# Encoder block, one core: three raw strips loaded a block earlier, the route block reordered with the first expert gather inside it, expert weight splits and a norm step moved, and unread products of the unit matrix put into TensorE's waits

## The chip, the cores and the metric

The kernel runs on one core of one Trainium2 chip. The metric is the time of one execution on the device, in microseconds (us); lower is better. The core has TensorE (PE in the profile; PEld is its weight load), VectorE (DVE), ScalarE (ACT), GpSimd (POOL) and SyncE (SP, which here only issues DMAs), and 16 DMA engines.

## The reference

A residual block over 4096 rows of width 1024, behind 16 meta rows: a norm, a mixer, a norm, a mixture of experts, a norm.

```python
h = _layernorm(jnp.concatenate([meta, x], axis=1), ln0_g, ln0_b)
mix = _mixer(h, w_in[l], ...)                      # 1024 -> 4352 wide projection, attention and convolution, w_o
h = _layernorm(alpha * h + mix, ln1_g[l], ln1_b[l])
ffn = _hier_moe(h, ...)
h = _layernorm(alpha * h + ffn, ln2_g[l], ln2_b[l])

# _hier_moe: the best of 4 groups, in it the best 2 of 8 experts
g_prob = softmax(xt @ w_rg + b_rg); g_top, g_idx = top_k(g_prob, 1)
e_top, e_loc = top_k((xt @ w_re + b_re) in the group g_idx, 2)
weight = g_top * softmax(e_top)
order = argsort(eid); sizes = bincount(eid, length=32)
xs = xt[tok[order]]
a = silu(ragged_dot(xs, w_gate, sizes)) * ragged_dot(xs, w_up, sizes)      # 1024 -> 512
ys = ragged_dot(a, w_down, sizes) * weight[order]                            # 512 -> 1024
out = zeros.at[tok[order]].add(ys)
```

Products must be as exact as fp32. The kernel gets that by splitting each fp32 operand into a rounded high part and the rest, and running three fp32r products (high by high, low by high, high by low) for each one of the reference.

## The kernel before

**Stages.** `mixer` begins with a prologue, a block of its own in which the meta rows go through the norm and the projection (its products are L564, on strips of `meta_raw`). The main block follows: 8 blocks of 512 rows (`BLOCKS`, `TOK`), each in 50 strips of weights (`N`); in the first block each strip is loaded raw from memory (`load_raw`, L636, into `raw`), its high part is made by ACT (`w_slot` L743) and its low part by DVE (L898), and it is stored split (`split_weights`), from where the later seven blocks load it. At the end of a block the eight transposes' groups that carry the next block's rows (`HX_AT`) stand one per strip. Behind the last block TensorE does for each of the last 4 row tiles `router_rows` (8 transposes) and `router_product`, and then `router_logits`; each waits for the norm's and the split's steps on DVE, POOL and ACT.

**route** turns the router's logits into lists. DVE chooses groups and experts (L84 to L122), TensorE counts them (`rank_rows`, L153 and L154, ahead of the semaphore `counted`), DVE works out the first tile of each expert (`bounds`, `tile_row`), each choice's place (`place_rows`, L169 to L174) and its weight (`weigh`, L135 to L147), writes 16 one-hot tables (L1441, L1443), which ACT scales (`listed`, L1386) and TensorE multiplies (`lists`, L1469). POOL gathers the records of the earlier blocks (`r_got`), TensorE turns them (`turned`, L1474), and DVE adds both into `row_index` (L1450 and on). SP meanwhile loads the first expert's weights (12 chunks of 512 KB: 4 gate, 4 up, 4 down), whose first 8 high parts ACT makes behind its `listed` (L1391).

**experts** runs 32 experts over 82 tiles of 128 gathered rows, laid out as a loop over the experts and in it a loop over the expert's tiles; 16 experts have 2 tiles, 12 have 3, 3 have 4 and one has 1. The engines run the same loop, joined only by semaphores. For tile `g`:

- TensorE: 24 gate products, 24 up products (each weight chunk serves 6), 8 transposes of the next tile's rows, 24 down products of tile `g-1`, 4 transposes of `prod`. Before the first tile's up products of an expert it waits for the low parts of its up chunks.
- ACT: Silu of the gate result (`act`, L1644), in an expert's last tile (`swap`) the high parts of the next expert's 4 gate chunks, the next rows' high parts (`xT_hi`), in the last tile the high parts of the 4 up chunks, `aT_hi`, in an expert's first tile the down chunks, and `measure(g-1)` (sum and sum of squares for the last norm, L1630 to L1634).
- DVE: in the last tile the 4 gate low parts of the next expert (L1673), `prod` (L1719), `xT_lo` (L1668), `normalise(g-2)` (L1688, L1693), in the last tile the 4 up low parts, `aT_lo` (L1726), `add_base(g-1)` (`both`, L1682, waits for the gathered `base`), in the first tile the 4 down low parts.
- POOL: `gather_rows(g+2)`, whose landing it waits for; `store_rows(g-2)`; `store_part(g-1)`; `deviation(g-1)` (two small steps that make 1/sigma of the norm, L1579 and L1582); a wait for the part's landing; `gather_base(g)`. `hold` is a wait in the instruction stream, so the order of these is the order of the code, and each index (`x_at`, `out_at`, `y_at`) is copied and waited for ahead of its DMA.
- SP: reloads each chunk for the next expert once its low part has been made, in the order gate, up, down.

Semaphores count; nothing is planned by a program. The order on each engine is that of the code.

## Time and profile before

| | us |
|---|---|
| median of 3 runs | 4194.5 |
| fastest and slowest of them | 4185.06 and 4198.86 |
| the profiled execution, its own time | 4199.52 |
| its span in the trace | 4197.5 |

The profiled execution took 2.0 us more than its span, and 5.0 us more than the median. The page gives each engine's busy time, the chain of work that ended last, and the costliest groups of instructions; the timeline gives single instructions with the idle time ahead of them and what ended it; the waits list who waited for whom; the windows give busy time and TensorE's granted clock by stretch (1.00 is 2.4 GHz, 0.50 is 1.2 GHz). "issue" as a releaser means that the profile shows no other engine that was waited for. The cuts used below: prologue 0 to about 62, mixer to about 2634, `route` to about 2662, `experts` to the end.

### The profile page before, as it was taken

How to read it: one execution, taken by the hardware profiler on the slowest of the kernel's cores; microseconds unless marked ns; L12 is line 12 of the kernel's file. 1: busy time of each engine (PE TensorE's matmuls, PEld its weight loads, DVE VectorE, ACT ScalarE, POOL GpSimd, SP SyncE). 2: the span in 40 equal slices, each digit the busy share in tenths (PEclk: the TensorE clock that was granted, in tenths of full speed). 3: DMA queues.
4: the chain of work that ended last, by engine and by line, in shares of the span. 5: the costliest groups of instructions: out<-in, count | busy, mean ns of one | idle time of the engine just before them, and what ended most of it. 6: DMA issues, size and time to landing. Idle time of an engine off the chain costs nothing. (4 is left out here: it accounts for less than half of the span.)

```text
span 4197.5 us, 60770 instructions
## 1 busy us (share of the span) xinstructions
PE 4076.5 (97%) x20066; PEld 3395.4 (81%) x20067; DVE 2073.1 (49%) x3202; ACT 1439.2 (34%) x2543; POOL 744.8 (18%) x1020
## 2 busy tenths in 40 slices
PE   8999999999999999999999998699999999999997
PEld 7888888888888888888888887587888888788886
DVE  3554443443443443443443444577656567665664
ACT  2422311311311311311311311366556456555553
POOL 2000010000000001001001001234333333433333
PEclk9999999999999999999999998799999999999998
DMA  8787456456456455456455555676756566665562
GB/s 251 241 306 244 145 202 204 156 198 196 159 199 195 166 200 187 169 197 187 175 197 184 175 197 186 217 254 222 252 187 205 188 219 229 228 211 190 195 218 81
DMA packets 278468, 840.53 MB, mean 200 GB/s; under 512 B 47952, under 2 KB 99408, under 8 KB 226688
## 3 DMA queue, kind: packets, MB, share of 16 engines
q1 hardware_dynamic: 228400, 716.61, 50.2%
q0 software_dynamic: 49936, 121.90, 8.7%
q8 instruction: 114, 1.87, 0.2%
q14 instruction: 18, 0.15, 0.0%
HBM read 717.60 MB, written 178.45 MB: 213 GB/s over the span
## 5 line engine op out<-in xcount | busy, mean ns | idle before, releaser
L1110 PE MATMUL bank<-hT_hi,w_slot 128*128 128x512 f32 x2176 | 862.3, 396 | 8.3 <-DVE w_slot L898 7.2
L1112 PE MATMUL bank<-hT_hi,w_slot 128*128 128x512 f32 x2176 | 848.9, 390 | 0.0
L1111 PE MATMUL bank<-hT_lo,w_slot 128*128 128x512 f32 x2176 | 848.1, 390 | 0.0
L1742 PE MATMUL e_bank<-e_w_hi,e_xT_hi 128*128 128x512 f32 x1312 | 522.7, 398 | 18.2 <-DVE e_xT_lo L1668 15.8
L1744 PE MATMUL e_bank<-e_w_hi,e_xT_lo 128*128 128x512 f32 x1312 | 514.7, 392 | 0.0
L1743 PE MATMUL e_bank<-e_w_lo,e_xT_hi 128*128 128x512 f32 x1312 | 513.9, 392 | 0.0
L1673 DVE TENSOR_TENSOR e_w_lo<-e_raw,e_w_hi 128x1024 fp32r<-128x1024 f32 x384 | 444.1, 1220 | 116.7 <-ACT e_w_hi L1624 116.7
L1110 PEld LDWEIGHTS bank<-hT_hi,w_slot 128*128 128x128 f32 x2176 | 409.0, 188 | 105.8 <-issue 24.6
L1112 PEld LDWEIGHTS bank<-hT_hi,w_slot 128*128 128x128 f32 x2176 | 408.9, 188 | 87.4
L1111 PEld LDWEIGHTS bank<-hT_lo,w_slot 128*128 128x128 f32 x2176 | 409.5, 188 | 81.2
L1624 ACT ACTIVATE e_w_hi<-e_raw 128x1024 fp32r<-128x1024 f32 x376 | 366.2, 1054 | 2.0 <-issue 2.0
L1742 PEld LDWEIGHTS e_bank<-e_w_hi,e_xT_hi 128*128 128x128 f32 x1312 | 248.3, 189 | 71.7 <-issue 22.5
L1744 PEld LDWEIGHTS e_bank<-e_w_hi,e_xT_lo 128*128 128x128 f32 x1312 | 248.1, 189 | 53.6
L1743 PEld LDWEIGHTS e_bank<-e_w_lo,e_xT_hi 128*128 128x128 f32 x1312 | 248.7, 190 | 50.0
L1742 PE MATMUL e_bank<-e_w_hi,e_aT_hi 128*128 128x512 f32 x664 | 266.5, 401 | 2.7 <-DVE e_both L1682 2.7
L52 POOL TENSOR_SCALAR rstd<-moments 128x1 f32<-128x1 f32 (+1 forms) x69 | 24.8, 359 | 1360.7 <-DVE moments L47 1360.7
L1744 PE MATMUL e_bank<-e_w_hi,e_aT_lo 128*128 128x512 f32 x664 | 260.3, 392 | 0.0
L1743 PE MATMUL e_bank<-e_w_lo,e_aT_hi 128*128 128x512 f32 x664 | 259.7, 391 | 0.0
L766 ACT ACTIVATE work<-bank 128x512 f32<-128x512 f32 x128 | 76.5, 598 | 506.9 <-PE bank L1112 506.9
L1110 PE MATMUL bank<-w_slot,mixT_hi 128*128 128x512 f32 x512 | 206.5, 403 | 0.0
L1630 ACT ACTIVATE e_ignored<-e_both 128x1024 bf16<-128x1024 f32 x83 | 87.5, 1054 | 343.8 <-DVE e_both L1682 343.8
L716 POOL COPY h_rows<-x_rows 128x1024 f32<-128x1024 f32 x32 | 33.2, 1042 | 953.9 <-PE bank L1122 941.2
(330 smaller groups left out, 6712.7 us busy)
## 6 DMA issues: line engine op xcount, KB each, us to landing
w_slot<-split_weights SPq DMA_DIRECT2D x353, 1024.0 KB, 4.8
e_raw<-in_w_exp_gate_dram SPq DMA_DIRECT2D x128, 512.0 KB, 6.0
e_raw<-in_w_exp_up_dram SPq DMA_DIRECT2D x128, 512.0 KB, 6.1
e_raw<-in_w_exp_down_dram SPq DMA_DIRECT2D x128, 512.0 KB, 5.4
split_weights<-w_slot SPq DMA_DIRECT2D x50, 1024.0 KB, 5.7
h_rows<-h_rows SPq DMA_DIRECT2D x64, 512.0 KB, 7.7
x_rows<-in_x_dram SPq DMA_DIRECT2D x32, 512.0 KB, 5.5
raw<-in_w_in_dram SPq DMA_DIRECT2D x30, 512.0 KB, 7.2
```

Source lines behind the costliest of these rows:

```text
L52: po.tensor_scalar(rstd[0:rows, :], moments[0:rows, 1:2], LN_EPS, None, ALU.add).then_inc(ln_rstd, 1)
L716: po.tensor_copy(h[:, i1, :], xs[:, i1, :]).then_inc(h_copied, 1)
L766: a.activation(w[:, 0:TOK], got, ACT.Sigmoid).then_inc(taken_act, 1)
L1110: pe.matmul(out, hi, x_hi, start=first, stop=False)
L1111: pe.matmul(out, hi, x_lo, start=False, stop=False)
L1112: return pe.matmul(out, lo, x_hi, start=False, stop=last)
L1624: a.activation(w_hi[:, c, :], raw[:, c, :], ACT.Copy).then_inc(split_count(e, c, True)[0], 1)
L1630: a.activation(ignored[:, :], both[:, :], ACT.Copy, accum_out=moments[:, 0, :]).then_inc(summed, 1)
L1673: v.tensor_tensor(w_lo[:, c, :], raw[:, c, :], w_hi[:, c, :].bitcast(FP32), ALU.subtract)\
L1742: pe.matmul(out_p, hi, x_hi, start=first, stop=False)
L1743: pe.matmul(out_p, hi, x_lo, start=False, stop=False)
L1744: return pe.matmul(out_p, lo, x_hi, start=False, stop=last)
```

## The change

1. **Prologue.** The first 3 raw strips are issued at the end of the prologue's SP queue and no longer at the head of the next block's. `meta_raw` moves to the slots' area so that `raw` is free.
2. **Mixer.** The eight groups of `HX_AT` stand in pairs, two at each second strip.
3. **route.** DVE weighs ahead of the wait for `counted`; the placing and the tables stand ahead of the writing of `bounds`; ACT makes 4 high parts ahead of `listed` and 4 behind; DVE makes 2 low parts (`done_early`) ahead of its wait for the lists; POOL gathers the first tile's rows inside `route` once `row_index`'s first column is written (`first_rows`), and no longer at the head of `experts`.
4. **experts, splits.** DVE makes the first expert's gate low parts 2 and 3 and the first `xT_lo` ahead of its six memsets. In the loop an expert's 4 up low parts move from the last tile of the expert ahead of it to the head of its own first tile; the 4 gate low parts are parted, 2 ahead of `prod` and 2 behind `xT_lo`.
5. **experts, norm.** POOL's `deviation(g-1)` moves behind `gather_base(g)`. ACT runs a Silu of one column into `e_unused` at the end of each tile.
6. **`keep_warm`.** TensorE runs fp32 products of the unit matrix by itself, 512 columns wide, into a bank that nobody reads: 6, 3, three times (2 and 2), and 1 behind the mixer (22 in all); 6, 7 and 7 in `route`; 2 behind the first transposes of `experts` and 3 ahead of the last down product. 47 in all, each number fixed.

```diff
+def keep_warm(pe, bank, ident, count):
+    for _ in range(count):
+        pe.matmul(bank[:, :], ident[:, :], ident[:, :].unsqueeze(1).to_broadcast([P, 4, P]), start=True, stop=True)
...
@@ mixer, prologue, sync
+                for s in range(RAW):
+                    for dst, src in strip_dmas(*strips[s], raw[:, s, :]):
+                        sp.dma_start(dst, src).then_inc(raw_in[s], 16)
@@ mixer
-        HX_AT = {WO0 - 1 + i: i for i in range(2 * TILES)}
+        HX_AT = {WO0 + 2 * i: (2 * i, 2 * i + 1) for i in range(TILES)}
...
-                for s in range(ahead):
-                    load_raw(s)
...
                 pe.wait_ge(hx_lo, BLOCKS * 2 * TILES + 1)
+                keep_warm(pe, pj[0], ident, 6)
                 pe.wait_ge(wo_taken, BLOCKS * 2 * TILES + 1)
                 for i in range(TILES):
+                    if i:
+                        keep_warm(pe, pj[0], ident, 2)
                     router_rows(BLOCKS, i)
+                    keep_warm(pe, pj[0], ident, 2 if i else 3)
                     router_product(BLOCKS, i)
+                keep_warm(pe, pj[0], ident, 1)
                 router_logits(BLOCKS)
@@ route, gpsimd
                 po.wait_ge(got_in, 16)
+                po.wait_ge(first_rows, 1)
+                po.tensor_copy(x_at[:, :], row_index[:, 2:3, 0]).then_inc(weights["x_at_set"], 1)
+                hold(po, weights["x_at_set"], 1)
+                po.indirect_dma_start(out=weights["rows"][:, :], out_offset=None, in_=h1[0:h1.shape[0] // 2, :],
...
@@ route, scalar
+                split_hi(range(weights["early"] // 2))
                 for j in range(2 * TILES):
...
-                for c in range(weights["early"]):
...
+                split_hi(range(weights["early"] // 2, weights["early"]))
@@ route, vector
+                v.wait_ge(exp_ready, 1)
+                weigh(v, link, r, tb)
                 v.wait_ge(counted, 1)
...
+                for c in range(weights["done_early"]):
+                    v.wait_ge(weights["hi_ready"], c + 1)
+                    v.tensor_tensor(weights["w_lo"][:, c, :], weights["raw"][:, c, :],
...
                 v.wait_ge(listed_up, 1)
@@ route, tensor
+                keep_warm(pe, spare_bank, tb["ident"], 6)
                 pe.wait_ge(both_ready, 1)
                 rank_rows(pe, r, tb, ranks, E).then_inc(counted, 1)
+                keep_warm(pe, spare_bank, tb["ident"], 7)
...
                 mm.then_inc(turned_up, 1)
+                keep_warm(pe, spare_bank, tb["ident"], 7)
@@ experts, gpsimd
-                gather_rows(0)
+                hold(po, rows_in, 16)
...
                     store_part(g - 1)
-                    deviation(g - 1)
                     hold(po, part_out, g * 16 + 16)
                     gather_base(g)
+                    deviation(g - 1)
@@ experts, scalar
                         measure(g - 1)
+                        a.activation(unused[:, :], minus_half[:, :], ACT.Silu)
@@ experts, vector
                 total = count_tiles(v)
+                for c in range(weights["done_early"], GC):
+                    split_lo(0, c)
+                evacuate(0)
...
-                for c in range(2 * GC):
-                    split_lo(0, c)
-                evacuate(0)
...
                     with v.Fori(lo, hi) as g:
+                        with v.If(g == lo):
+                            for c in range(GC, 2 * GC):
+                                split_lo(e, c)
                         with v.If(g == swap):
-                            for c in range(GC):
+                            for c in range(GC // 2):
                                 split_lo(e + 1, c)
...
                         evacuate(g * 2 + 2)
+                        with v.If(g == swap):
+                            for c in range(GC // 2, GC):
+                                split_lo(e + 1, c)
                         normalise(g - 2)
-                        with v.If(g == swap):
-                            for c in range(GC, 2 * GC):
-                                split_lo(e + 1, c)
@@ experts, tensor
                 transposes(16)
+                keep_warm(pe, bank[3], ident, 2)
...
+                keep_warm(pe, bank[3], ident, 3)
                 down(total - 1)
```

Three places as the instructions stand on their engines. DVE in the experts' loop, from `xT_lo` to the first of the two `both` of a tile, before; `e_w_lo` is a low part, the branches are the tests for the last and the first tile:

```order
L1668 TENSOR_TENSOR e_xT_lo<-e_bank,e_xT_hi 128x512
L1688 SCALAR_TENSOR_TENSOR e_done<-e_both,e_minus_mean,e_gain 128x1024
...
L1693 SCALAR_TENSOR_TENSOR e_finished<-e_done,e_rstd,e_shift 128x1024
L1722 COMPARE_AND_BRANCH
L1672 ISA
L1673 TENSOR_TENSOR e_w_lo<-e_raw,e_w_hi 128x1024
...
L1726 TENSOR_TENSOR e_aT_lo<-e_bank,e_aT_hi 128x512
...
L1682 SCALAR_TENSOR_TENSOR e_both<-e_bank,slot_weight,e_base 128x512
```

The same engine in the changed kernel, from the start of an expert to `prod`:

```order
L1559 TENSOR_LOAD bounds
L1559 ISA x2
L1743 UNCONDITIONAL_BRANCH
L1744 COMPARE_AND_BRANCH
L1702 ISA
L1703 TENSOR_TENSOR e_w_lo<-e_raw,e_w_hi 128x1024
...
L1744 UNCONDITIONAL_BRANCH
L1747 COMPARE_AND_BRANCH
...
L1703 TENSOR_TENSOR e_w_lo<-e_raw,e_w_hi 128x1024
...
L1752 TENSOR_TENSOR e_prod<-e_bank,e_act 128x512
```

The up low parts (under L1744) now stand behind the read of the new expert's `bounds`, which itself stands behind both `both` of the tile ahead.

POOL in the experts' loop, from the part's store to the end of a tile, before and then changed:

```order
L1572 DMA h_rows<-e_both,e_y_at 9216x1024
L1579 TENSOR_SCALAR e_rstd<-e_moments 128x1
L37 REGISTER_ALU
L1582 TENSOR_TENSOR e_rstd<-e_rstd,minus_half 128x1
L37 ISA
L1563 ISA
L1563 COPY e_y_at<-row_index 128x2
L1566 DMA e_base<-h_rows,e_y_at 128x1024
```

```order
L1601 DMA h_rows<-e_both,e_y_at 9216x1024
L37 ISA
L1592 ISA
L1592 COPY e_y_at<-row_index 128x2
L1595 DMA e_base<-h_rows,e_y_at 128x1024
L1608 TENSOR_SCALAR e_rstd<-e_moments 128x1
L37 REGISTER_ALU
L1611 TENSOR_TENSOR e_rstd<-e_rstd,minus_half 128x1
```

The two steps on `e_rstd` went from ahead of the wait (`L37`) for the part's landing to behind the base's DMA, at the end of the tile.

TensorE in `route`, changed (`L44` is `keep_warm`); before, the same rows stand without those of `L44`:

```order
L44 MATMUL r_spare_bank<-ident 128x512 x6
L159 MATMUL r_ranks<-lr_both,before 128x128
L160 MATMUL r_ranks<-lr_both,ones 128x128
L44 MATMUL r_spare_bank<-ident 128x512 x7
L1496 MATMUL r_lists<-r_listed,r_hot_lo 128x196 x8
L1501 MATMUL r_turned<-ident,r_got 128x128 x2
L44 MATMUL r_spare_bank<-ident 128x512 x7
```

The count of `r_ranks` now stands behind six of the unread products, and the lists behind seven.

## Rows read from the trace of the kernel before

**Rows 1.** The page: an engine's busy time and share, the chain's lines.

```profile
PE 4076.5 (97%) x20066; PEld 3395.4 (81%) x20067; DVE 2073.1 (49%) x3202; ACT 1439.2 (34%) x2543; POOL 744.8 (18%) x1020
...
DMA e_rows<-h_rows,e_x_at 8%; DMA h_rows<-e_both,e_y_at 7%; PE e_bank L1742 2%; PE e_bank L1744 2%; PE e_bank L1743 2%; POOL out_dram L1588 1%; DVE e_w_lo L1673 1%; POOL e_out_at L1586 1%; POOL e_y_at L1563 1%; DMA e_base<-h_rows,e_y_at 1%; POOL e_x_at L1555 1%; PE e_bank L1751 0%; ACT e_ignored L1630 0%; POOLq L37 0%; DVE e_both L1682 0%
```

**Rows 2.** Windows: stretch, its length, busy time of PE (x count), then PEclk.

```profile
200.00:2500.00 2300.00, 2298.98 (x11642) 1.00 0.57 193
2640.00:2653.00 13.00, 3.22 (x12) 0.50 1.02 390
2676.00:2681.00 5.00, 5.00 (x14) 0.54 1.03 404
2700.00:4170.00 1470.00, 1444.16 (x6787) 1.00 0.62 210
```

**Rows 3.** Timeline (start, length, instruction, idle before), end of the prologue.

```profile
51.65 2.72 PE L564 MATMUL bank<-work,meta_raw 128*128 128x16 f32 x12
...
55.09 4.18 SPq L636 DMA_DIRECT2D raw<-in_w_in_dram  x4
...
61.62 0.76 PE L1110 MATMUL bank<-hT_hi,w_slot 128*128 128x512 f32 x1 [7.25 <-DVE w_slot L898]
```

**Rows 4.** Waits of PE between 2600 and 2640: total us, times, longest.

```profile
PE bank L1130 <- DVE router_rowsT_lo L865: 10.0, 4, 4.1
```

**Rows 5.** Timeline of `route` and the start of `experts`.

```profile
2640.69 0.74 DVE L160 COPY lr_earlier<-base 128x32 f32<-128x32 f32 x1 [1.28 <-PE r_ranks L154]
...
2647.57 0.17 DVE L135 TENSOR_REDUCE lr_gsum<-lr_gexp 128x4 f32<-128x16 f32 x1
...
2649.34 0.27 DVE L1441 TENSOR_SCALAR r_hot_hi<-r_count_up,r_tile_of 128x98 f32<-128x98 f32 x1
...
2650.43 4.30 PE L1469 MATMUL r_lists<-r_listed,r_hot_lo 128*128 128x196 f32 x16 [9.78 <-ACT r_listed L1386]
...
2662.67 0.18 POOL L1555 COPY e_x_at<-row_index 128x1 int32<-128x1 int32 x1 [16.93 <-POOLq L1355]
...
2668.05 1.97 PE L1751 MATMUL e_bank<-ident,e_rows 128*128 128x128 f32 x8 [13.09 <-DMA e_rows<-h_rows,e_x_at]
...
2675.52 0.79 PE L1742 MATMUL e_bank<-e_w_hi,e_xT_hi 128*128 128x512 f32 x1 [5.50 <-DVE e_xT_lo L1668]
```

**Rows 6.** Waits of PE, DVE and POOL in the experts' loop, 2700 to 4170.

```profile
PE e_bank L1742 <- DVE e_xT_lo L1668: 10.3, 9, 1.2
PE e_bank L1787 <- DVE e_prod L1719: 9.2, 7, 2.9
...
DVE e_both L1682 <- DMA e_base<-h_rows,e_y_at: 88.7, 36, 5.6
...
POOL e_rstd L1579 <- ACT e_ignored L1634: 24.2, 20, 4.7
```

**Rows 7.** Timeline of PE, POOL and DVE from expert 5's first tile on.

```profile
2856.71 0.48 PE L1742 MATMUL e_bank<-e_w_hi,e_xT_hi 128*128 128x512 f32 x1
...
2857.93 1.58 POOL L1566 DMA_INDIRECT e_base<-h_rows,e_y_at  x1 [0.85 <-POOL e_y_at L1563]
...
2858.49 4.62 DVE L1673 TENSOR_TENSOR e_w_lo<-e_raw,e_w_hi 128x1024 fp32r<-128x1024 f32 x4
...
2863.63 1.40 DVE L1682 SCALAR_TENSOR_TENSOR e_both<-e_bank,slot_weight,e_base 128x512 f32<-128x512 f32 x2
...
2872.30 0.19 POOL L1579 TENSOR_SCALAR e_rstd<-e_moments 128x1 f32<-128x1 f32 x1
2872.64 0.57 POOL L1582 TENSOR_TENSOR e_rstd<-e_rstd,minus_half 128x1 f32<-128x1 f32 x1
...
2874.16 0.19 POOL L1563 COPY e_y_at<-row_index 128x2 int32 x1 [0.95 <-DMA h_rows<-e_both,e_y_at]
```

**Rows 8.** Groups by line, 2700 to 4170: ACT's table load in the loop.

```profile
L1644 ACT ACT_TABLE_LOAD x81 | 103.9, 1283 | 44.4 <-issue 43.5
```

**Rows 9.** Timeline of DVE at the kernel's end.

```profile
4181.86 1.41 DVE L1682 SCALAR_TENSOR_TENSOR e_both<-e_bank,slot_weight,e_base 128x512 f32<-128x512 f32 x2 [4.44 <-DMA e_base<-h_rows,e_y_at]
```

More of the change, by code:

```diff
@@ L326, in mixer @@
         raw = place([weights + 4 * 6 * D], "raw", [P, RAW, D])
-        meta_raw = place([weights + 4 * 4 * D], "meta_raw", [P, META_RAW, D])
+        meta_raw = place([weights], "meta_raw", [P, META_RAW, D])
         at = [weights + 4 * 8 * D]
@@ L357, in mixer @@
         tp = banks[6:8]
+        raw_in = [sem(f"raw_in{i}") for i in range(RAW)]
         with ExitStack() as c1, nc.Block() as block:
@@ L364, in mixer @@
             gains_in = sem1("gains_in")
-            raw_in = [sem1(f"meta_raw_in{i}") for i in range(META_RAW)]
+            meta_raw_in = [sem1(f"meta_raw_in{i}") for i in range(META_RAW)]
             ln_step, ln_moments, ln_rstd, ln_gained, ln_done = (
@@ L566, in _ @@
                     mm.then_inc(pj_ready, 1)
-        raw_in = [sem(f"raw_in{i}") for i in range(RAW)]
         x_in = [sem(f"x_in{i}") for i in range(TILES)]
@@ L826, in block_of_strips @@
                             take_rows(b, RT_AT[s])
-                        if s in HX_AT:
-                            q = HX_AT[s]
+                        for q in HX_AT.get(s, ()):
                             a.wait_ge(hx_ready, b * 2 * TILES + q + 1)
@@ L1071, in block_of_strips @@
                             place_rows(v, route_link, r, tb, tb["region"]).then_inc(slots_ready, 1)
-                        if s in HX_AT:
-                            q = HX_AT[s]
+                        for q in HX_AT.get(s, ()):
                             v.wait_ge(hx_hi, b * 2 * TILES + q + 1)
@@ L1270, in block_of_strips @@
                             rank_rows(pe, r, tb, quad[2], E).then_inc(counted, 1)
-                        if s in HX_AT:
-                            q = HX_AT[s]
+                        for q in HX_AT.get(s, ()):
                             pe.wait_ge(ln_done, b * LNS + TILES + q // 2 + 1)
@@ L1314, in load_expert_chunk, with route @@
     sp.dma_start(dst, expert_chunk(t, e, c)).then_inc(weights["raw_in"][c], 16)
-def route(nc, t, tb, records, keep, weights):
+def route(nc, t, tb, records, h1, keep, weights):
     G, E = t["w_rg"].shape[1], t["w_re"].shape[1]
@@ L1338, in route @@
         upto, first, spare = sb("r_upto", [P, E]), sb("r_first", [P, E]), sb("r_spare", [P, E])
+        start = sb("r_start", [P, E])
         tile_row_f, tile_row = sb("r_tile_row_f", [P, 1]), sb("r_tile_row", [P, 1], I32)
@@ L1344, in route @@
         got = sb("r_got", [P, P, 2])
-        ranks, lists, turned = [ctx.enter_context(nc.psum_tensor(name, [P, TOK], FP32))
-                                for name in ("r_ranks", "r_lists", "r_turned")]
+        ranks, lists, turned, spare_bank = [ctx.enter_context(nc.psum_tensor(name, [P, TOK], FP32))
+                                            for name in ("r_ranks", "r_lists", "r_turned", "r_spare_bank")]
         tables, step = sem("r_tables"), sem("r_step")
@@ L1388, in _ @@
                     ins.then_inc(worth_made, 1)
-                for c in range(weights["early"]):
-                    a.wait_ge(weights["raw_in"][c], 16)
-                    a.activation(weights["w_hi"][:, c, :], weights["raw"][:, c, :], ACT.Copy)\
-                     .then_inc(weights["hi_ready"], 1)
+                split_hi(range(weights["early"] // 2, weights["early"]))
             @block.vector
@@ L1423, in _ @@
                 v.tensor_tensor(tile_row[:, :], tile_row_f[:, :], tile_no[:, :], ALU.add).then_inc(tile_rows_ready, 1)
+                link(v.tensor_scalar(start[:, :], first[:, :], float(P), None, ALU.mult))
+                link(v.tensor_tensor(r["earlier"][:, :, :], r["earlier"][:, :, :],
+                                     ranks[:, 0:TILES * E].rearrange("p (t e) -> p t e", e=E), ALU.add))
+                link(place_rows(v, link, r, tb, start))
+                v.tensor_scalar(in_tile_i[:, :], tb["slot"][:, :], P - 1, None, ALU.bitwise_and)
+                link(v.tensor_scalar(tile_of_i[:, :], tb["slot"][:, :], P.bit_length() - 1, None, ALU.arith_shift_right))
+                v.tensor_copy(in_tile[:, :], in_tile_i[:, :])
+                link(v.tensor_copy(tile_of[:, :], tile_of_i[:, :]))
+                for j in range(2 * TILES):
+                    v.tensor_scalar(hot_hi[:, j, :], count_up[:, 0:MT], tile_of[:, j:j + 1], None, ALU.is_equal)\
+                     .then_inc(hi_made, 1)
+                    v.tensor_scalar(hot_lo[:, j, :], count_up[:, :], in_tile[:, j:j + 1], None, ALU.is_equal)\
+                     .then_inc(lo_made, 1)
                 v.tensor_copy(bounds[:, 0, :], first[:, :])
@@ L1824, in encoder_block @@
                        raw_in=[ctx.enter_context(nc.semaphore(f"e_raw_in{c}")) for c in range(chunks)],
+                       rows=sb("e_rows", [P, D]), x_at=x_at,
                        hi_ready=ctx.enter_context(nc.semaphore("e_hi_ready")),
+                       lo_ready=ctx.enter_context(nc.semaphore("e_lo_ready")),
+                       rows_in=ctx.enter_context(nc.semaphore("e_rows_in")),
+                       x_at_set=ctx.enter_context(nc.semaphore("e_x_at_set")),
                        consts_in=ctx.enter_context(nc.semaphore("e_consts_in")))
-        route(nc, t, tb, records, keep, weights)
+        route(nc, t, tb, records, h1, keep, weights)
         experts(nc, t, h1, out2, keep, weights, tb)
```

47 lines of the change are left out of this document (22 added, 25 removed).

## The prediction

> **What bounds the kernel now.** The page first: TensorE is busy 97% of the span, and yet most of the chain that ended last is DMA waits of POOL's gathers and stores, 8% and 7% [rows 1]. The windows by stretch say where TensorE is not the bound. From 200 to 2500 us it is busy 2298.98 of 2300 us at full clock, so nothing that other engines do in the mixer's main blocks can move the time. In the experts' loop, 2700 to 4170, it is busy 1444.16 of 1470 us [rows 2]; the tiles that nothing disturbs are 17.7 us long there, which is 72 products of 0.227 us, twelve short transposes and little else. 82 such tiles would take 1452 us; they take 1492 (2675.52 to about 4168), so 40 us are lost, of which the waits name 10.3 for `xT_lo` and 9.2 for `prod` [rows 6]; the rest is clock drops and ends. The other places are the gap of 7.25 us behind the prologue [rows 3], the mixer's tail [rows 4], and `route` with the first tile's start: 2634 to 2675.52 [rows 5], with the clock at 0.50 and 0.54 of full for most of it [rows 2].
>
> **Prologue: minus 4.0 us.** The last meta products end at 54.4, SP issues the raw strips at 55.09, and the first product follows at 61.62, 6.5 us behind the issue [rows 3]. Issued earlier, the strip is there when the block opens, and ACT's and DVE's splits (1.06 and 1.23 us) with their handovers remain: first product near 57.6. Gain 61.6 - 57.6 = 4.0, between 3 and 4.5.
>
> **HX_AT: 0 to 1 us gained.** The main blocks have 1 us idle in 2300 us [rows 2]. Pairs save some switches between product kinds; I take 0.3.
>
> **Mixer's tail: 0.** TensorE waits four times for DVE's `router_rowsT_lo`, 10.0 us in all [rows 4], and about 6 us for the last norm. What keeps DVE late is its own row of norm steps, which is untouched. The 22 unread products lie in these waits. Their cost: 16 records of 196 columns took 4.30 us, 0.27 each, on a clock of 0.50 that rose near their end [rows 2, 5]. Two records of 512 columns are then 2 x 0.27 x 512/196 = 1.4 us at that mean; I estimate 0.9 at full and 1.8 at half clock. Two of them fit a wait of 2.5 to 4 us; if they don't, they put off TensorE by under 1 us at each of four places. 0 to plus 2 us, I take 0.
>
> **route and the first tile: minus 14 us.** Three steps. (a) `weigh`, 2647.57 to 2649.34, moves into DVE's wait for the count, which ends with L160 at 2640.69 and 1.28 us of waiting [rows 5]: 1.8 us earlier, less 0.5 by which it overruns the wait, and the 0.4 of `bounds`. The lists come 1.5 us earlier. (b) The first rows' index was copied at 2662.67, behind the block's end, and the rows reached TensorE at 2668.05 [rows 5]. The copy now follows `row_index` at about 2655, so the rows are there near 2660.5 and TensorE's transposes start when `experts` opens, near 2661 instead of 2668.05. From there ACT's and DVE's split of them gives a first product at 2664.4: in the trace 7.5 us lay between, because DVE still had 8 low parts to make [rows 5]; now 2 are done and 2 stand ahead, and 3.4 us remain. 2675.5 - 2664.4 = 11.1. (c) 12 products ran at 0.43 us before the clock rose (5.00 us for 14 records at 0.54 [rows 2]); with the unread products ahead they run at 0.23, which saves 2.4. Together 13.5; against it, six unread products at half clock (1.8 each, from 2634 on) can hold the count, due at 2639.4, for 1 to 3 us. Range 10 to 15, I take 13.5 with up to 3 of it open.
>
> **The end: minus 0.7.** The last `both` waits at 4181.86 for the base [rows 9], which the part's store and `deviation` stand ahead of; with `deviation` behind it, it is issued 0.7 us sooner. The three products ahead of the last down product save TensorE a stretch at half clock, but this wait hides it.
>
> Front and end together: 4.0 + 0.3 + 13.5 + 0.7 = **18.5 us gained.**
>
> **The loop, up low parts: this is what decides.** TensorE needs the first up chunk's low part 24 x 0.227 = 5.45 us into an expert's first tile. Before, DVE had made all four before that: it starts them 1.8 us into the tile (2858.49 against 2856.71), ahead of `aT_lo` and `both` [rows 7], the first being ready at 3. Now they stand behind `both`, and so behind the base's landing. Two bounds. Without any wait for the base: `normalise` ends about 2.5 us into the tile (it ended at 1.8; two low parts less stand ahead of `prod`, which comes sooner, two stand behind `xT_lo`), then `aT_lo` 0.65, both 1.4, reading the new bounds 1.1, the first low part 1.15: 6.8, a stall of 1.3 us. 31 changes of expert give 40 us. With the base as it lands now: it is issued 1.22 us into the tile at 2857.93 [rows 7] and takes 4.8 us in the median of all of its DMAs, so `both` starts at 6.0 at the earliest, the low part is ready at 9.7, and TensorE stalls 4.2. Over the 31 changes (their rows are those of L1566 and L1742 like the two shown) the issue lies between 8 us ahead of the tile and 1.4 us into it; 10 changes give the floor of 1.3, the other 21 give their landing less 1.85, and the sum is 81 us. DVE's 36 waits for the base, 88.7 us [rows 6], show that it is late often; before, TensorE had until 10 us into the tile before that reached it.
>
> **The loop, deviation.** Its two steps (0.19 and 0.57 us, from 2872.30 to 2873.21) lay under the part's landing, which ended at 2874.16 [rows 7]. Behind the base they add 0.9 us with the hold to POOL's own row of steps, and that row is already as long as TensorE's tile: by the mean of all tiles 18.2 us of index copies, issues and landings, with 0.9 us of it waiting for others. Nothing is queued behind the base but the next tile's row gather, whose landing POOL waits for, and so the next base. If POOL sets the pace everywhere this is 82 x 0.9 = 74 us; if TensorE's stalls let POOL catch up, or where an expert's middle tiles leave it 3 us, it is nothing by itself. What it saves is the wait for ACT's sum, 24.2 us [rows 6]. It acts through the base, so it adds to the stalls above and not beside them.
>
> **Taken together.** The stalls are 40 at least and 81 with today's base. A stalled TensorE makes POOL's next base earlier by comparison, which pulls to the floor; `deviation` pulls to the top. I take 67. Against it, the first two low parts fewer ahead of `prod` remove the waits for `prod` and `xT_lo`, 9.2 + 10.3 [rows 6], and some 3 us of low clock behind them: 22. **Net 45 us lost**, between 15 (40 less 25) and 90 (81 and some 10 of `deviation`).
>
> Clock: stalls of 2 us in an otherwise full tile were followed by a fall to half speed in three of four cases of this trace, each costing 1.7 us; where POOL sets the pace it costs nothing more. It is inside the range.
>
> **ACT's Silu into `e_unused`.** ACT loads a table ahead of each tile's Silu, 81 times 1.283 us [rows 8]. On ACT's row of the changed kernel this load still stands in the loop ahead of the Silu; the added Silu costs 0.2 us at a place where ACT waits. By this row nothing is gained: 0. The Trainium skill (ScalarE: Activation LUTs, What ACT_TABLE_LOAD costs) says the load is a real instruction placed when compiling and that a switch costs its 1283 ns and a drain of about 1380 ns; the trace agrees with the first number. If the switch were avoided by that rule, Silu would come up to 2.7 us earlier, which no term of the sum uses.
>
> **The sum.** 4199.5 (profiled) - 18.5 + 45 = 4226; against the median of 4194.5, 5.0 below that execution, **4221 us**. The case's own range: 4194.5 - 15 + 90 = 4269 down to 4194.5 - 18.5 + 15 = 4191.
>
> **Rivals.** (1) The stalls don't come, the front's gain stays: *faster*. The mechanism is the base: if it lands within 3 us of the tile's start and DVE's reading of the bounds costs little, the first up part is ready at 5.5. It decides at 1.8 us: every `both` that ends 3.2 us into the tile or sooner costs nothing. For it: in 10 of 31 changes the base is there by then, and half as many splits stand ahead of `prod`. Against: the others, and `deviation`. Then the loop only gains its 22 us or less: 4194.5 - 18.5 - 10 = 4166. (2) A wash: stalls at the floor, 40 less 22, against 18.5: 4194.5 - 0.5, about 4195. (3) POOL sets the pace: its row grows by 0.9 in each tile and the 24.2 isn't saved; 74 + 22 against 18.5: 4194.5 + 77, about 4272. (4) The unread products do harm: 13 of them at half clock ahead of the count and the lists, 5 us late; it only adds to one of the others, 5 us.
>
> **Chances.** Forecast 0.55, of which nearly all lies over 4207; (1) 0.20; (2) 0.15; (3) 0.10. A difference of under 0.3% (12.6 us) can't be told from none: faster 0.20, same 0.16, slower 0.64. The range reaches into (1) and up to (3): **4168 to 4270**.
>
> **What would show it.** Right: first main product near 57.6; first expert product near 2664 at full clock; waits of TensorE's up products for `e_w_lo` (L1703 then), some 30 of 1 to 5 us; no wait for `prod`; POOL's `rstd` steps directly behind the base, and POOL's wait for ACT's sum gone. Wrong: no such waits or of under 1 us each in sum under 20 us; or a first expert product after 2668; or the loop's tiles longer without a wait for `e_w_lo`, which would be POOL's rows.

## The result, and the profile after

The changed kernel takes 4224.2 us in the median of 7 runs (4215.6 to 4238.9), the kernel before, run beside it, 4189.3 us (4177.1 to 4198.9). The ratio is 1.0082, with a 95% interval of 1.0060 to 1.0103: slower by 25 to 43 us. 4221 had been forecast.

The profiled execution of the changed kernel took 4216.7 us, its span is 4214.7, 17.2 us more than the span of before. It is one of the shorter ones of this kernel, whose median is 7.5 us more, while the traced execution of before (4199.5) was longer than any of the seven timed beside the changed kernel. What follows splits up these 17.2 us; the other 18 of the medians' distance are in executions that have no trace.

The page, in the form of [rows 1], TensorE's line and the chain:

```profile
PE 4114.6 (98%) x20160; PEld 3410.8 (81%) x20161; DVE 2081.8 (49%) x3202; ACT 1448.9 (34%) x2625; POOL 702.4 (17%) x1020
...
PE e_bank L1775 7%; PE e_bank L1776 7%; PE e_bank L1777 7%; DMA h_rows<-e_both,e_y_at 2%; DVE e_w_lo L1703 1%; PE e_bank L1784 1%; ACT e_w_hi L1653 1%; DMA e_rows<-h_rows,e_x_at 1%; DVEq L1559 1%; DMA e_base<-h_rows,e_y_at 1%; PE e_bank L1821 1%; DVE e_both L1712 0%; DVE e_done L1718 0%; ACT e_ignored L1659 0%; ACT L1673 0%
```

The chain now gives POOL's gathers and stores 1% and 2% of the span (8% and 7% before) and the experts' products 21%. POOL stopped being what the end was followed back to, and the kernel got slower: a chain tells who came last, not what would be saved.

The windows as in [rows 2], TensorE's busy time and granted clock:

```profile
200.00:2500.00 2300.00, 2299.42 (x11660) 1.00 0.57 193
2630.00:2653.00 23.00, 21.89 (x56) 0.89 0.87 325
2661.00:2681.00 20.00, 20.00 (x91) 0.96 0.74 269
2700.00:4130.00 1430.00, 1385.32 (x6475) 0.99 0.62 210
```

In `route` the clock is now 0.89 of full (0.50 before), which the unread products do (0.56 without them, in e4), and in the 20 us from 2661 on, the first tile's start, 0.96; in its first 5 us alone (2661.5 to 2666.5) it is 0.90, where before had 0.54. In the loop TensorE is busy 1385.3 of 1430 us; the same cut of before gives 1405.6.

The waits of TensorE from 2660 on, in the form of [rows 6]: total us, times, longest.

```profile
PE e_bank L1775 <- DVE e_w_lo L1703: 45.5, 31, 7.1
PE e_bank L1775 <- DVE e_both L1712: 0.2, 1, 0.2
```

31 waits for the up low parts, one for each change of expert; those for `xT_lo` and `prod` are gone. The same of DVE and of POOL:

```profile
DVE e_w_lo L1703 <- issue: 54.8, 31, 3.3
...
DVE e_finished L1723 <- POOL e_rstd L1611: 16.1, 10, 3.0
...
DVE e_both L1712 <- DMA e_base<-h_rows,e_y_at: 10.4, 8, 2.0
```

```profile
POOL e_x_at L1584 <- PE e_bank L1784: 103.6, 63, 11.3
...
POOL e_rstd L1608 <- ACT e_ignored L1663: 4.3, 2, 3.1
```

The base makes DVE wait 10.4 us in all, where it was 88.7 [rows 6]. What is new is 54.8 us of "issue" ahead of the first up low part, 31 times: the read of the next expert's bounds. From its first register load to the low part it takes 2.5 us in the median; DVE's idle time in it is 0.84 to 3.26 us, 2.0 in the median, less where `both` is still running when it begins. POOL waits 103.6 us for TensorE's transposes (21.6 before); it is ahead and doesn't set the pace. One of the common changes of expert, tile start at 3302.63, on DVE and TensorE:

```profile
3302.23 1.28 DVE L1723 SCALAR_TENSOR_TENSOR e_finished<-e_done,e_rstd,e_shift 128x1024 f32<-128x1024 f32 x1 [0.27 <-DVE e_done L1718]
3303.54 0.69 DVE L1759 TENSOR_TENSOR e_aT_lo<-e_bank,e_aT_hi 128x512 fp32r<-128x512 f32 x1
3304.15 1.40 DVE L1712 SCALAR_TENSOR_TENSOR e_both<-e_bank,slot_weight,e_base 128x512 f32<-128x512 f32 x2
3307.83 4.63 DVE L1703 TENSOR_TENSOR e_w_lo<-e_raw,e_w_hi 128x1024 fp32r<-128x1024 f32 x4 [2.28 <-issue]
```

```profile
3302.63 0.47 PE L1775 MATMUL e_bank<-e_w_hi,e_xT_hi 128*128 128x512 f32 x1
...
3307.96 0.39 PE L1777 MATMUL e_bank<-e_w_hi,e_xT_lo 128*128 128x512 f32 x1
3309.11 0.50 PE L1775 MATMUL e_bank<-e_w_hi,e_xT_hi 128*128 128x512 f32 x1 [0.77 <-DVE e_w_lo L1703]
```

`both` ends at 3305.55, DVE then idles 2.28 us in the read, the first low part is there at 3309.05, 6.4 us into the tile, and TensorE waited 0.77. The base was in time. 24 of the 31 tiles behind a change of expert look like this, 18.4 to 19.0 us long, though in nine of them `both` ends only 4.0 us into the tile and the idle time is 0.8 to 0.9: in all 24 the low part starts 4.9 to 5.4 us into the tile. The other seven are 22.4 to 27.6 us long. In five of them `finished` waits for rstd and then `both` for the base; in the longest, at 2910.69, the base is in time, but the one-tile expert's four down low parts stand ahead of the read; in the one at 2697.51 the gate low parts are late, which waited 3.69 us for ACT's high parts. One of the five, at 3225.57:

```profile
3227.07 1.28 DVE L1723 SCALAR_TENSOR_TENSOR e_finished<-e_done,e_rstd,e_shift 128x1024 f32<-128x1024 f32 x1 [0.92 <-POOL e_rstd L1611]
...
3230.78 1.41 DVE L1712 SCALAR_TENSOR_TENSOR e_both<-e_bank,slot_weight,e_base 128x512 f32<-128x512 f32 x2 [1.83 <-DMA e_base<-h_rows,e_y_at]
3234.44 4.63 DVE L1703 TENSOR_TENSOR e_w_lo<-e_raw,e_w_hi 128x1024 fp32r<-128x1024 f32 x4 [2.25 <-issue]
```

```profile
3235.72 0.65 PE L1775 MATMUL e_bank<-e_w_hi,e_xT_hi 128*128 128x512 f32 x1 [4.44 <-DVE e_w_lo L1703]
...
3238.72 0.63 PE L1776 MATMUL e_bank<-e_w_lo,e_xT_hi 128*128 128x512 f32 x1
3239.15 0.48 PE L1777 MATMUL e_bank<-e_w_hi,e_xT_lo 128*128 128x512 f32 x1
3239.46 0.40 PE L1775 MATMUL e_bank<-e_w_hi,e_xT_hi 128*128 128x512 f32 x1
```

`finished` waited 0.92 us for rstd, `both` 1.83 for the base, the read took 2.25, TensorE stood still for 4.44, and its next eight products ran at half clock (0.43 us from start to start instead of 0.23), 1.6 us more. Over all 31 changes the tiles are 67.7 us longer than undisturbed ones: 45.5 are the waits, 12 are products at half clock behind the seven long stalls, and the rest is 0.3 us or so at each restart.

By kind of tile, the excess, which is the time over the undisturbed 17.71 us (from the starts of the tiles' first products). By the changes of expert in the trace 15 experts have 2 tiles and 13 have 3, not 16 and 12, which makes the 82. "First" counts the loop's own first tile, and the loop's last tile is in no row.

| tiles | before | after |
|---|---|---|
| first of an expert, 31 | 11.9 | 67.4 |
| last of an expert, 30 | 23.8 | -0.9 |
| middle, 19 | 0.2 | -0.6 |
| the one-tile expert | 4.7 | 0.8 |
| loop, first product to the end of the last transposes | 1493.0 | 1519.3 |

The whole line of events, and what each stretch gave:

| | before | after | change of the stretch |
|---|---|---|---|
| first product of the main blocks | 61.6 | 59.6 | -2.0 |
| last product of the main blocks | 2597.8 | 2592.1 | -3.6 |
| `route` starts | 2634.2 | 2629.4 | +0.9 |
| first expert product | 2675.5 | 2661.5 | -9.3 |
| last transposes of `prod` end | 4168.5 | 4180.8 | +26.2 |
| end | 4197.5 | 4214.7 | +4.9 |

### The profile page after: what moved, and what is told of

It is laid out like the page before. It is cut to its first block and busy times, and to the rows that moved or that the text cites. A ratio compares the mean times of both kernels' runs of the same rounds, so it can differ in the third digit from the quotient of the medians.

```text
span 4214.7 us, 61133 instructions
## 1 busy us (share of the span) xinstructions
PE 4114.6 (98%) x20160; PEld 3410.8 (81%) x20161; DVE 2081.8 (49%) x3202; ACT 1448.9 (34%) x2625; POOL 702.4 (17%) x1020
## 5 line engine op out<-in xcount | busy, mean ns | idle before, releaser
L1775 PE MATMUL e_bank<-e_w_hi,e_xT_hi 128*128 128x512 f32 x1312 | 529.0, 403 | 45.5 <-DVE e_w_lo L1703 45.5
L1031 DVE TENSOR_TENSOR work<-bank,work 128x512 f32<-128x512 f32 x64 | 44.3, 692 | 314.5 <-PE bank L1117 250.1
L1117 PE MATMUL bank<-w_slot,mixT_lo 128*128 128x512 f32 x512 | 199.6, 390 | 0.0
```

Source lines behind the costliest of these rows:

```text
L1031: v.tensor_tensor(work[2][:, 0:TOK], got, work[0][:, 0:TOK], ALU.mult).then_inc(taken, 1)
L1117: return pe.matmul(out, lo, x_hi, start=False, stop=last)
L1775: pe.matmul(out_p, hi, x_hi, start=first, stop=False)
```

## The experiments

All ratios are against the kernel before, timed beside them on the same chip, with a 95% interval.

| run | what | ratio | interval | loop, us |
|---|---|---|---|---|
| the changed kernel | | 1.0082 | 1.0060 to 1.0103 | 1519.3 |
| e1_up_back | up low parts back | 0.9998 | 0.9988 to 1.0008 | 1492.1 |
| e2_dev_back | `deviation` back | 1.0051 | 1.0033 to 1.0069 | 1513.0 |
| e3_both_back | both back | 0.9998 | 0.9986 to 1.0011 | 1485.5 |
| e4_no_warm | no unread products | 1.0119 | 1.0099 to 1.0140 | 1529.4 |
| e5_up_alone | before, up low parts late | 1.0165 | 1.0143 to 1.0186 | 1544.7 |
| e6_dev_alone | before, `deviation` late | 1.0029 | 1.0018 to 1.0040 | 1496.7 |
| e7_up_ahead_of_both | up ahead of `both`, `deviation` back | 1.0030 | 1.0017 to 1.0043 | 1503.9 |
| e8_up_ahead_of_read | up ahead of the read | 1.0131 | 1.0109 to 1.0154 | 1548.2 |
| e9_gather_back | e3, first gather in `experts` | 0.9992 | 0.9982 to 1.0003 | 1499.3 |
| e10_both_back_no_warm | e3, no unread products | 0.9994 | 0.9982 to 1.0006 | 1506.3 |
| e11_read_dev_back | e8, `deviation` back | 1.0132 | 1.0116 to 1.0148 | 1537.8 |
| e12_gate_whole | all gate low parts ahead of `prod` | 1.0177 | 1.0163 to 1.0190 | 1575.6 |

The loop's length is that of the one traced execution and moves by some 10 us between executions of a kernel; the ratios decide.

**The two moves, put back one by one (e1, e2, e3).** e1:

```diff
                     with v.Fori(lo, hi) as g:
-                        with v.If(g == lo):
-                            for c in range(GC, 2 * GC):
-                                split_lo(e, c)
...
                         normalise(g - 2)
+                        with v.If(g == swap):
+                            for c in range(GC, 2 * GC):
+                                split_lo(e + 1, c)
```

> The changed kernel with the 4 up low parts back in the expert's last tile, behind `normalise`. Theory A (the place of the up low parts makes the loop's loss: TensorE waited 45.5 us for them, 31 times, and some 20 us more went on half clock behind the stalls): the waits for e_w_lo go, the loop (1519 us in the changed kernel's profile, 1493 before) falls to 1480 to 1495, and the time to 4183 to 4198. Theory B (POOL with `deviation` behind the base sets the loop's pace): the loop stays within 8 us of 1519 and the waits turn up for prod, rows or both; the time stays over 4210.

e2:

```diff
                     store_part(g - 1)
+                    deviation(g - 1)
                     hold(po, part_out, g * 16 + 16)
                     gather_base(g)
-                    deviation(g - 1)
```

> The changed kernel with `deviation` back ahead of the wait for the part's landing, all else as changed. Theory A: POOL had slack (it waited 103.6 us for TensorE's transposes), so the time stays within 5 us of the changed kernel's 4224, and POOL's wait for ACT's sum returns. Theory B: the loop falls by 15 us or more, time under 4210.

e3 has both.

> Both put back: prologue, pairs of transposes, route, parted gate low parts, Silu and unread products stay. Theory A: like the run with only the up low parts back, within 5 us, so 4170 to 4195, with the first expert product near 2661 (2675 before). Theory B: 10 us or more below that run.

e1 comes down to 4192.5 us, the time of before, as theory A has it; e3 is the same, 4192.4. e2 came to 4212.3, ratio 1.0051: 13 us better than the changed kernel, more than the 5 that A allowed, less than the 15 of B. So the place of the up low parts makes the whole loss against before. `deviation` adds about a third of it while they are late (the two intervals, 1.0033 to 1.0069 and 1.0060 to 1.0103, just overlap), and with them put back it adds nothing (e1 against e3). TensorE's waits in e1:

```profile
PE e_bank L1777 <- DVE e_xT_lo L1698: 10.5, 17, 0.9
PE e_bank L1777 <- DVE e_w_lo L1703: 6.8, 11, 1.5
...
PE e_bank L1823 <- DVE e_prod L1751: 3.6, 3, 3.0
```

45.5 us of waits for `e_w_lo` became 6.8, and those for `xT_lo` that the change had removed are back, 10.5 us.

**Each move alone on the kernel before (e5, e6).** The edits are those of the two diffs above, the other way round, on the kernel before.

> The kernel before with one edit: the 4 up low parts of an expert at the head of its own first tile. Theory A (the place alone makes the loss, whatever else is changed): waits for e_w_lo about 31 times, most of them 0.8 to 2 us, some of 4 us and more where the base is late; all 4 gate low parts still stand ahead of prod, so each stall is a little longer than in the changed kernel; the loop 1493 becomes 1515 to 1545, time +25 to +50 us against before. Theory B (it only costs together with the late `deviation`): within 12 us of before.

> The kernel before with one edit: `deviation` behind the base's gather. The runs so far: with the up low parts back it made nothing (both read 0.9998), with them late it made 0.3%. Theory A (it costs only where something stands behind normalise that TensorE waits for soon): within 8 us of before, POOL's wait for ACT's sum gone, a new wait of DVE for rstd of 80 to 200 us that reaches TensorE hardly anywhere. Theory B (it lengthens POOL's row by 0.9 us a tile and POOL sets the pace): +20 us or more.

e5 takes 1.65% more, 69 us, above the range of A: the place alone costs more than the whole change. e6 takes 0.29% more, 12 us, between the two theories; here `deviation` costs something without late up low parts, unlike in e1 against e3. Its waits on DVE, beside POOL's:

```profile
DVE e_finished L1693 <- POOL e_rstd L1582: 124.6, 54, 5.9
...
DVE e_both L1682 <- DMA e_base<-h_rows,e_y_at: 12.8, 17, 3.4
```

The expected wait for rstd is there, 124.6 us in 54 waits, and it takes the place of the wait for the base (88.7 in [rows 6], 12.8 here). The 74 us of a POOL that sets the pace are not there; that `deviation` acts by moving `normalise`, and with it what stands behind it on DVE, fits these waits, but e1 has a wait of the same size for rstd (137.0 us) and loses nothing, so where the 12 us come from is not shown.

**Why the changed kernel loses less than e5 (e12).** The 4 gate low parts whole again:

```diff
                         with v.If(g == swap):
-                            for c in range(GC // 2):
+                            for c in range(GC):
                                 split_lo(e + 1, c)
...
-                        with v.If(g == swap):
-                            for c in range(GC // 2, GC):
-                                split_lo(e + 1, c)
                         normalise(g - 2)
```

> The changed kernel with all 4 gate low parts ahead of prod again. The up move alone on the kernel before cost 69 us, in the changed kernel the loop loses less. If the parting of the gate low parts is what saves (prod and xT_lo come 2.3 us sooner in an expert's last tile): the loop 1519 becomes 1530 to 1550, and the waits in the last tiles (excess 0 in the changed kernel, 24 us before) come back in part; time 4232 to 4250. If not: within 6 us of 4224.

4267.0 us, 17 us over the range: the parting is worth 0.95%, 40 us, in this kernel. The last tiles' excess is 4.0 us against -0.9, which is what was expected of it, in part: nearly all of the 23.8 of before stay away. The first tiles' excess is 113.8 against 67.4, which wasn't expected: 19 of the 31 tiles behind a change are longer than 19 us, against seven. DVE waits 100.7 us for rstd and 37.9 for the base there. The read is hardly longer: of the 104.0 us of "issue" ahead of low parts, 39.6 are seven waits of 5.66 ahead of the gate low parts, and the 31 reads make 64.

**Is it the read of the bounds? (e8, e11).** The up low parts behind `both`, still in the last tile:

```diff
                         add_base(g - 1)
+                        with v.If(g == swap):
+                            for c in range(GC, 2 * GC):
+                                split_lo(e + 1, c)
                         with v.If(g == lo):
```

> The changed kernel with the up low parts behind both, but still in the last tile, ahead of the next expert's read of its bounds. In the changed kernel DVE spent 2.25 us on that read between both and the first low part at most changes of expert. If the read is what makes the common stall of 0.8 us, 24 of the 31 stalls go and the 7 long ones get 2.2 us shorter: e_w_lo waits 45 fall to 15 to 28, time 25 to 35 us below the changed kernel, 4190 to 4200. If the late base makes most of the loss, it falls by less than 15.

It fell the other way: 4249.8 us, 1.31% over before and 0.5% over the changed kernel. Where the base was in time the stall of 0.8 us is indeed gone: 4 of the 31 first tiles last 17.68 us, none in the changed kernel. But the others wait longer, 66.5 us in all. The trace showed a wait of DVE for rstd of 225.9 us, so e11 put `deviation` back as well.

> Up low parts behind both but ahead of the next expert's read, as in the run that took 1.3% more than before, and now with `deviation` back ahead of the wait. There DVE waited 225.9 us, 61 times, for rstd. Theory A (in that run the late rstd held normalise, and with it both and the up low parts): DVE's wait for rstd falls under 20 us, the waits for e_w_lo from 66 to 20 to 40, and the time by 30 us or more, to 4195 to 4220. Theory B (the place ahead of the read is bad by itself): it stays over 4235.

Theory A fell too. The wait for rstd is gone, and the time is the same, 1.0132. DVE's waits in e11, and then POOL's DMAs by the page's list of issues (the number is the median us to landing) of the changed kernel and of e11:

```profile
DVE e_both L1712 <- DMA e_base<-h_rows,e_y_at: 135.0, 49, 4.6
```

```profile
h_rows<-e_both,e_y_at POOLq DMA_INDIRECT x82, 3.5
```

```profile
h_rows<-e_both,e_y_at POOLq DMA_INDIRECT x82, 7.1
```

The wait for the base took rstd's place, 135.0 us. And the part's store, which POOL waits for ahead of the base's gather, lands after 7.1 us in the median instead of 3.5 (3.4 in e2, which differs from e11 in the up low parts' place alone). The reload of the up chunks, which SP issues when their low parts are made, begins 7.9 us into a tile in e8 and e11 (8.3 in e12), 6.3 in the changed kernel and 3.2 in the one before (medians of the first of the four, from the issues' rows). All three kernels whose reload begins later than 7.5 have a slow store (6.1, 7.1, 6.4), and the eleven with 6.3 or less have 3.4 to 5.0. In e11 the 30 stores in tiles with such a reload take 7.5 us in the median, the 52 others 5.0; in e12 it is 7.0 and 4.7, in e8 6.3 and 5.9. But the store itself moved too: it is issued 3.8 us into the tile in the changed kernel (median), ahead of the reload, and 9.3, 10.5 and 7.5 in e11, e8 and e12. That the reload's traffic delays the store fits all of this; it was not tried by itself (a kernel with the same DVE order and another time of reload would tell), so it stays an explanation.

**Up low parts ahead of `both` (e7).**

```diff
                                         aT_hi[:, :, :].bitcast(FP32), ALU.subtract).then_inc(a_ready, 1)
+                        with v.If(g == swap):
+                            for c in range(GC, 2 * GC):
+                                split_lo(e + 1, c)
                         add_base(g - 1)
```

> The changed kernel with the up low parts in the last tile between aT_lo and both, and `deviation` back. If what costs is standing behind both and the read of the bounds, no wait for e_w_lo is left and the loop is 1475 to 1490, like or a little below the run with both put back (1486): time 4180 to 4195. If any place behind normalise costs, it stays over 4200.

1.0030, 12.6 us over before: much better than behind `both` or behind the read, but still a loss, and 14 us above the 4195 of its first theory; it stays over 4200, as the other one (any place behind `normalise` costs) has it. 8.7 us of waits for `e_w_lo` are left (13, none over 0.9), and 11.0 us for the rows, which e3 has at 5.4. No order of DVE that was tried does better than the one of before.

**The unread products (e4, e10).** All lines of `keep_warm` taken out, of the changed kernel and of e3.

> The changed kernel without any of the 47 unread products. Theory A (they buy clock): the clock is at half through route and into the first tile, as before; the count of the choices comes 2.9 us sooner, the first rows 0.7 us sooner, and the first 12 to 14 products cost 0.43 instead of 0.23 us: the time is 0 to 4 us above the changed kernel's 4224. Rival (they stand in the way of the count and of the block's end): 2 to 6 us below it. A difference of 20 us or more would say that they disturb the loop, which neither expects.

> Both moves put back and no unread products. Taking them out of the changed kernel cost 15 us (1.0119 against 1.0082), 10 of them inside the loop, where there are none. Theory A (the loop's part of that comes from the stalls, whose length depends on how far POOL is behind at the start; without stalls it isn't there): 2 to 7 us above the run with both back (4192), all of it ahead of the loop and in its first tile. Theory B (they matter to the loop by themselves): 12 us or more.

e4 takes 15 us more than the changed kernel (the intervals touch, 1.0060 to 1.0103 and 1.0099 to 1.0140), 10 of them in the loop, where experts 3 to 5 stall longer. e10 is the same as e3 within 0.1%: A, or a little below it. Its trace shows why nothing is left: counted from the last product of the main blocks, the count of the choices comes 2.2 us sooner without them (42.3 instead of 44.5 us behind it), yet the first expert product 0.3 us later (69.1 and 68.7), and the first tile is 1.5 us longer on its slower clock: 1.8 us in all, which is less than the medians can tell. A good part of what they give by the clock they take by standing ahead of the count.

**The first gather in `route`, and the kernel's end (e9).**

```diff
-                x_at = weights["x_at"]
-                po.wait_ge(first_rows, 1)
...
-                hold(po, rows_in, 16)
+                gather_rows(0)
                 gather_base(-1)
```

> As the run with both put back, but the first rows are gathered at the head of experts again, as before, not in route. It tells two things apart: the gather's own worth (first rows at TensorE 2658 there; I expect 2662 to 2664 here, so 4 to 6 us later) and the kernel's end, where POOL's drain behind the last store took 9.30 us in all five kernels with the gather in route and 0.47 before. If the gather in route makes the long drain, it is back at 0.5 and the end is 6 to 9 us shorter, the time the same or up to 4 us less; if not, 9.3 stays and the time is 4 to 6 us more.

Both parts came out. The last store's issue in the changed kernel and in e9, with the span of each ahead:

```profile
core 0 of [0], span 4214.7 us
...
4200.79 0.18 POOL L1615 COPY e_out_at<-row_index 128x1 int32 x1 [1.64 <-DVE e_finished L1723]
4201.83 1.06 POOL L1617 DMA_INDIRECT out_dram<-e_finished,e_out_at  x1 [0.85 <-POOL e_out_at L1615]
```

```profile
core 0 of [0], span 4196.8 us
...
4189.07 0.18 POOL L1608 COPY e_out_at<-row_index 128x1 int32 x1 [1.64 <-DVE e_finished L1716]
4192.75 1.07 POOL L1610 DMA_INDIRECT out_dram<-e_finished,e_out_at  x1 [3.50 <-issue]
```

From the index of the last store to the end it is 13.9 us in the changed kernel and 7.7 in e9. Ten traced kernels gather in `route`, and in each POOL's drain behind the last store takes 9.30 us by the trace's record of it; in the four that don't (before, e5, e6, e9) it takes 0.47, with some 3 us more ahead of the store's issue. The gather itself brings the first expert product from 2668.7 in e9 to 2661.8 in e3, 6.9 us, and the end gives back 6: the two kernels are the same within their intervals. What the drain waits for, the runs don't show.

## Why the prediction was right, point by point

- **Sign and size.** Slower, 4221 forecast, 4224.2 measured. The mechanism named as deciding decided: with the up low parts back the loss is gone (e1, 0.9998), and they alone cost more than all of it (e5). But two sizes were off and offset each other: front and end were to gain 18.5 us and gained 9.1 in the traces (2.0 + 3.6 - 0.9 + 9.3 - 4.9), the loop was to lose 45 and lost 26.2. And the medians lie 35 apart, the spans 17, against a forecast of 26.5. That the time came within 3 us is luck in part.
- **Prologue, -4.0: -2.0.** SP's part was right; ACT's first split runs from 55.38 to 56.44. But DVE starts its first low part only at 57.54: at the block's head it works off 14 semaphore increments (L888 to L899 of the changed kernel, 56.23 to 57.46 in the trace's records), which before lay under the wait for the strip (56.02 to 57.25, with the low part at 60.29). That is 1.1 us. The low part then took 1.92 us, where the rows before have 1.23, and POOL's copies (55.40 to 60.37) now run beside it: 0.7 more. The nearest row had been taken without asking what the engine had ahead of it and who else was at work.
- **HX_AT, -0.3: the main blocks are 3.6 us shorter.** Over all traces the stretch from their first to their last product is 2535.8 to 2536.2 us in the three kernels without the change's mixer, and 2531.4 to 2534.5 in the eleven with it. The bound of 1 us was wrong; whether the pairs or the moved buffers do it was not separated.
- **Mixer's tail, 0: +0.9.** Inside the bound of 0 to 2.
- **route and first tile, -13.5: -9.3, and 1.9 in the first tile by the clock, -11.2 together.** Inside 10 to 15. The named deduction was real: the six unread products took 8.23 us from 2629.45 and held the count to 2637.5, some 3 us late, though `weigh` hid most of it (DVE's wait for the count is 0.24 us). The last seven run to 2655.8, but by the trace's records the block ended with POOL's drain, at 2656.6.
- **The end, -0.7: +4.9.** The late `deviation` gave 1.1 us (e6 against before, from the start of the last down product: 25.1 and 26.2). The drain took 6 and was in no row of before.
- **Up low parts, 67 us of stalls: 67.7 of excess at the 31 changes.** The sum is right and its make-up isn't. The waits themselves are 45.5. The read of the bounds was taken at 1.1 us behind `both`, and DVE idles 2.0 in the median; the base, which was to be late at 21 of 31 changes, was late at five and made DVE wait 10.4 us in all; and 12 of the 67 are half clock, which no term had. The 24 common tiles, with the base in time, make 20.5 us, where the floor of 1.3 each gives 31: TensorE waits 0.5 to 1.0 us in each, as `normalise` ended sooner (0.9 or 2.1 us into the tile, not 2.5).
- **The late base is the step that failed.** The landings of before were laid beside the new order as if POOL's would stay; but a longer tile gives POOL time, and it waited 103.6 us for TensorE's transposes (21.6 before). The text had said so as a pull toward the floor, and then took a value in the middle.
- **What the change takes away, 22: 41.** All 40.6 us of excess that the loop had before are gone or counted again in the first tiles; the last tiles went from 23.8 to -0.9. The prediction credited the parted gate low parts with this, but either move takes most of it: e5 and e12, with them whole, have 6.9 and 4.0 left, e3, with them parted and the up low parts back, 3.3. This term, mis-sized by half, is why the loop lost 26 and not 45.
- **`deviation`: as a rival (POOL's pace) wrong, as a push on the base small.** It costs 13 us beside late up low parts, 12 alone, nothing in e1. The path is in part another: in the long tiles DVE's `normalise` waits for rstd first (0.6 to 2.0 us in five of them), and then `both` for the base.
- **ACT's Silu: 0.** The trace has the table load 82 times at 1.283 us, as before, and the added Silu at 0.187 us each where ACT waits; no run takes it out by itself. The Trainium skill (ScalarE: Activation LUTs, What ACT_TABLE_LOAD costs) has the same 1283 ns; the trace agrees, also in that the load stays where it was placed.

## What to carry to other kernels

A step moved to "just before it is needed" inherits the lateness of all that now stands ahead of it on its engine, down to the register reads at a loop's head and the semaphore increments at a block's: count those too, from a row of the same place. When a change makes the main engine slower, the engines that were late catch up, so their lateness may not be added to the new stall. And look at what the kernel's end costs when a DMA moves to another block: of the 7 us won at the front 6 were lost there.

## What the runs showed of the hardware that was not expected

- POOL's final drain takes 0.47 us in four kernels and 9.30 us in ten, to the same hundredth in each group, and the groups are told apart by one indirect gather 1.5 ms earlier, in another block (e9 against e3).
- A DVE subtraction with two operands in memory on chip, 1.22 us alone (61.57 in the changed kernel), took 1.92 and 2.05 us beside POOL's copies, of which one took 2.03 instead of 1.04. They end one behind the other, as if taking turns: a copy at 58.38, the first subtraction at 59.47, the next copy at 60.37, the second subtraction at 61.44.

```profile
57.54 3.90 DVE L904 TENSOR_TENSOR w_slot<-raw,w_slot 128x1024 fp32r<-128x1024 f32 x2 [7.87 <-ACT w_slot L750]
...
61.57 1.22 DVE L904 TENSOR_TENSOR w_slot<-raw,w_slot 128x1024 fp32r<-128x1024 f32 x1
```

  The Trainium skill (SBUF — State Buffer, SBUF: two separate sides) says that such a DVE operation and a GpSimd operation that reads there lock a shared pair of ports for a whole instruction; the trace agrees, in that both get longer and end in turn.
- The read of three loop bounds ahead of an inner loop holds DVE's next instruction back by 2.5 us from the first register load (median of 31); each load is 0.30 us in most. Where low parts are queued ahead of it, as in e8, it runs beside them and shows no idle time.
- Another place for four low parts of each expert moved the median landing of a store that they don't touch from 3.4 to 7.1 us (e2 and e11), with the store issued later in the tile.
